# Token stream of the latent attention: its projections in a new order, with norms and rotations next to matmuls

## The reference, cut to what matters

```python
def _mla_q(h, w_dq, q_norm, w_uq, rows, cols):
    q = (_rms_norm(h @ w_dq, q_norm) @ w_uq).reshape(b, s, MLA_HEADS, MLA_NOPE + MLA_ROPE)
    q_nope, q_pe = q[..., :MLA_NOPE], q[..., MLA_NOPE:]
    q_pe = _rope_2d(q_pe, rows, cols)                     # token stream only
    return jnp.concatenate([q_nope, q_pe], -1)

def _mla_kv(h, w_dkv, kv_norm, w_ukv, rows, cols):
    ckv = h @ w_dkv
    c_kv, k_pe = ckv[..., :MLA_KV_RANK], ckv[..., MLA_KV_RANK:]
    kv = (_rms_norm(c_kv, kv_norm) @ w_ukv).reshape(b, s, MLA_HEADS, MLA_NOPE + MLA_V)
    k_nope, v = kv[..., :MLA_NOPE], kv[..., MLA_NOPE:]
    k_pe = _rope_2d(k_pe[:, :, None, :], rows, cols)      # token stream only
    k = jnp.concatenate([k_nope, jnp.broadcast_to(k_pe, (b, s, MLA_HEADS, MLA_ROPE))], -1)
    return k, v

# second block, layer 0: h = x * (1 + sc1) + sh1, and after the mixer
# x = layer_norm(alpha * x + g1 * y); softmax(q k^T * scale) v runs over context and token keys
```

## Time and profile before

| | |
|---|---|
| median of 3 runs | 2492.07 us |
| lowest, highest | 2491.98, 2493.27 us |
| profiled execution, its own time | 2489.5 us |
| span of the profiled execution | 2487.7 us |
| mean granted PE clock over the span | 0.954 |

### The profile page before, as it was taken

One profiled execution on the slowest core, in us unless ns is written; L12 is line 12 of the kernel. 1 busy time (PEld: TensorE's weight loads), 2 busy tenths in 40 slices (PEclk: granted clock), 3 DMA queues, 4 the chain that ended last, 5 costly groups with the idle time before them and its releaser, 6 DMA issues.

```text
span 2487.7 us, 29431 instructions
## 1 busy us (share of the span) xinstructions
PE 2161.0 (87%) x12748; PEld 1181.7 (48%) x12748; DVE 677.1 (27%) x1303; ACT 216.7 (9%) x507; POOL 41.3 (2%) x109
## 2 busy tenths in 40 slices
PE   8988889888768878878878876987889999999998
PEld 6544353333323334334334333434657776646775
DVE  1332211321310120120120123122444434165344
ACT  1221110000100000000000000002310000060000
POOL 0000000000000000000000000000000003000000
PEclk9999998989899999999999999998999999999999
DMA  8879999999999999999999999994337554424550
GB/s 321 328 291 396 420 408 424 424 423 422 424 421 418 416 420 414 416 420 413 414 421 416 414 424 422 391 417 179 132 100 226 183 189 161 154 75 144 168 171 34
DMA packets 154819, 799.52 MB, mean 321 GB/s; under 512 B 15587, under 2 KB 71626, under 8 KB 101634
## 3 DMA queue, kind: packets, MB, share of 16 engines
q1 hardware_dynamic: 144504, 783.43, 78.2%
q10 hardware_dynamic: 10186, 14.16, 1.7%
HBM read 795.40 MB, written 7.19 MB: 323 GB/s over the span
## 4 chain that ended last, share of the span: by engine, by line
PE 69%; DMA 17%; DVE 8%; issue 3%; ACT 2%; SPq 1%; ACTq 0%; DVEq 0%
PE ps L288 12%; PE ps L1992 9%; DMA ring<-in_mlp_w 8%; PE ps L2451 8%; PE ps L2443 8%; PE ps L321 6%; PE ps L1960 5%; PE ps L2162 4%; PE ps L1965 3%; PE ps L2013 2%; PE ps L2001 2%; DVE expert_work L2035 2%; DMA ring<-in_w_up 2%; DMA ring<-in_na_w_qkv 2%; DMA ring<-in_w_gate 2%
## 5 line engine op out<-in xcount | busy, mean ns | idle before, releaser
L1960 PE MATMUL ps<-ring,xe 128*32 128x512 f32 x2048 | 295.0, 638 | 80.7 <-DMA ring<-in_w_up 29.3
L1992 PE MATMUL ps<-ring,expert_work 128*32 128x512 f32 x1408 | 238.2, 691 | 11.8 <-ACT expert_work L2022 11.0
L1965 PE MATMUL ps<-ring,xe 128*32 128x256 f32 x2048 | 206.9, 462 | 6.0 <-issue 6.0
L1965 PEld LDWEIGHTS ps<-ring,xe 128*32 128x32 f32 x2048 | 74.9, 110 | 174.7 <-issue 174.0
L1960 PEld LDWEIGHTS ps<-ring,xe 128*32 128x32 f32 x2048 | 61.7, 114 | 186.2 <-issue 94.0
L1992 PEld LDWEIGHTS ps<-ring,expert_work 128*32 128x32 f32 x1408 | 59.7, 122 | 156.1 <-issue 132.8
L2162 PE MATMUL ps<-ring,c_qT 128*128 128x512 f32 x256 | 114.1, 598 | 12.1 <-DMA ring<-in_mlp_w 12.1
L2154 PE MATMUL ps<-hT,ring 128*128 128x256 f32 x512 | 115.0, 383 | 6.6 <-DMA ring<-in_mlp_w 6.6
L2451 PE MATMUL ps<-ring,mlp_x_h 128*128 128x512 f32 x256 | 112.3, 592 | 0.0
L2451 PE MATMUL ps<-ring,mlp_n_h 128*128 128x512 f32 x256 | 112.3, 592 | 0.0
L2154 PEld LDWEIGHTS ps<-hT,ring 128*128 128x128 f32 x512 | 96.2, 190 | 28.7 <-DMA ring<-in_mlp_w 11.0
(11 more groups left out here) (425 smaller groups left out, 2448.1 us busy)
## 6 DMA issues: line engine op xcount, KB each, us to landing
ring<-in_w_gate SPq DMA_DIRECT2D x128, 1408.0 KB, 16.8
ring<-in_w_up SPq DMA_DIRECT2D x128, 1408.0 KB, 17.4
ring<-in_w_down SPq DMA_DIRECT2D x112, 1536.0 KB, 22.8
ring<-in_mlp_w SPq DMA_DIRECT2D x96, 1024.0 KB, 8.1
ring<-in_ada_w SPq DMA_DIRECT2D x32, 1536.0 KB, 10.2
ring<-in_na_w_qkv SPq DMA_DIRECT2D x20, 1024.0 KB, 13.7
ring<-in_w_in SPq DMA_DIRECT2D x8, 1536.0 KB, 18.7
ring<-in_w_down SPq DMA_DIRECT2D x16, 512.0 KB, 23.5
```

What stands on the lines that cost most here:

```text
L1960: nc.tensor.matmul(ps[32 * j:32 * j + 32, up, :], xe[:, k, :], w[:, :, 4 * j:4 * j + 4], start=(k == 0), stop=(k == KC - 1))
L1965: last = nc.tensor.matmul(ps[32 * j:32 * j + 32, 2, 256 * up:256 * up + 256], xe[:, k, :], two, start=(k == 0 and not up), stop=(k == KC - ...
L1992: last = nc.tensor.matmul(ps[32 * j:32 * j + 32, 1 - half, :], hgT[:, at:at + 32], w[:, (c - c0) * D + 512 * half:(c - c0) * D + 512 * hal ...
```

## The change

The context stream's program stays as it is. For the token stream each engine gets one function of its own, and five things differ.

1. The query latent is normed alone: `square` of `cq` follows its evacuation, with a root for two columns, and the key/value latent gets a second, later norm. The junk output of the squares goes to `kT`.
2. `run_c` is split. `run_cq` (8 transposes of `cq`) uses banks 4 to 7 and waits for "norm_q" alone. `run_ckv` (6 transposes of `ckv`, `kpe`) uses banks 4 to 6.
3. `run_uq` is split. Its first 8 jobs run ahead of `run_ckv`, its last 2 jobs after it in banks 7 and 0. `run_ukv` follows in banks 4, 5, 6, 1, 2, 3.
4. `spread` gives all evacuations of `run_uq` and `run_ukv` to ACT: 22 of them, where ACT had 11.
5. DVE does the key/value norm, the key rotation, the gain on `x` and both rotations of `qpe` while PE runs the up projections. The key rotation's scratch is `va`.

```diff
-                self.run_c = Run(transposes(4, lambda t, c: cq[:, t, c * P:(c + 1) * P], lambda c: cqT[:, c, :],
+                queries_turned = transposes(4, lambda t, c: cq[:, t, c * P:(c + 1) * P], lambda c: cqT[:, c, :],
...
+                if s:
+                    self.run_c = Run(queries_turned + latents_turned, banks)
+                else:
+                    self.run_cq = Run(queries_turned, (4, 5, 6, 7))
+
+                def spread(i, out, scale=None, cols=None):
+                    if s:
+                        return turn(i, out, scale, None, cols)
+                    return to_act(out, 1.0 if scale is None else scale, 0.0, cols), "act"
...
-                self.run_uq = Run(jobs, banks)
+                if s:
+                    self.run_uq = Run(jobs, banks)
+                else:
+                    self.run_uq_most = Run(jobs[:8], banks)
+                    self.run_ckv = Run(latents_turned, (4, 5, 6))
+                    self.run_uq_rest = Run(jobs[8:], (7, 0))
...
-                self.run_ukv = Run(jobs, banks)
+                self.run_ukv = Run(jobs, banks if s else (4, 5, 6, 1, 2, 3))
...
+            def tokens_pe(self, pe, normed):
+                self.run_t.pe(pe, normed)
+                self.run_t.finished(pe)
+                self.run_d.pe(pe)
+                pe.wait_ge(self.v.sem, self.v.at("norm_q"))
+                self.run_cq.pe(pe)
+                self.run_cq.finished(pe)
+                self.run_d.finished(pe)
+                self.run_uq_most.pe(pe)
+                pe.wait_ge(self.v.sem, self.v.at("norms"))
+                self.run_ckv.pe(pe)
+                self.run_uq_most.finished(pe)
+                self.run_uq_rest.pe(pe)
+                self.run_ckv.finished(pe)
+                self.run_ukv.pe(pe)
+                self.run_uq_rest.finished(pe)
+                self.run_ukv.finished(pe)
+                pe.wait_ge(self.v.sem, self.v.at("rope_q"))
+                self.run_q.pe(pe)
+
+            def tokens_act(self, act):
+                cq, ckv, a, v = self.buf["cq"], self.buf["ckv"], self.a, self.v
+                junk = view(self.buf["kT"], 1, Q_RANK)[:, 0, :]
...
+                self.run_t.ev(act, "act")
+                for t in range(NT):
+                    self.run_d.ev(act, "act", t, t + 1)
+                    self.run_d.out_of(act, t)
+                    square(t, cq[:, t, :])
+                root(0, "var_q", "sd_q")
+                for t in range(NT):
+                    self.run_d.ev(act, "act", 2 + t, 3 + t)
+                    self.run_d.out_of(act, 2 + t)
+                    square(2 + t, ckv[:, t, 0:KV_RANK])
+                self.run_cq.ev(act, "act")
+                root(2, "var_kv", "sd_kv")
+                self.run_uq_most.ev(act, "act")
+                self.run_ckv.ev(act, "act")
+                self.run_uq_rest.ev(act, "act")
+                self.run_ukv.ev(act, "act")
+                self.run_q.ev(act, "act")
+
+            def tokens_dve(self, dve):
...
+                self.run_t.ev(dve, "dve")
+                self.run_d.ev(dve, "dve", 0, NT)
+                invert(0, Q_RANK, "sq1", "var_q", "sd_q")
+                for t in range(NT):
+                    last = nc.vector.tensor_scalar(cq[:, t, :], cq[:, t, :], small[:, t:t + 1], None, ALU.mult)
+                last.then_inc(v.sem, v("norm_q"))
+                self.run_d.ev(dve, "dve", NT)
+                self.run_cq.ev(dve, "dve")
+                invert(2, KV_RANK, "sq3", "var_kv", "sd_kv")
...
+                last.then_inc(v.sem, v("norms"))
+                dve.wait_ge(ln_loaded.sem, ln_loaded.n)
+                for t in range(NT):
+                    nc.vector.tensor_tensor(x[:, t, :], x[:, t, :], lnb[:, 0, :], ALU.mult)
+                self.run_ckv.ev(dve, "dve")
+                self.run_uq_most.finished(dve)
+                self.run_uq_rest.finished(dve)
...
+                last.then_inc(v.sem, v("rope_q"))
```

90 lines of the change are left out of this document (39 added, 51 removed).

## The result

The changed kernel takes 2479.4 us (median of 4 executions, 2476.7 to 2483.5) against 2492.7 us for the kernel before (median of 4, 2492.0 to 2494.1). The forecast was 2474.3 us with a range from 2470.5 to 2480.5.

A forecast was written before the change was run, and what follows sets the result against it. TensorE, busy for 87% of the span, was taken as the bound. The stage's terms sum to 46.3 us in place of 64.1, giving 2471.7 us profiled and, with 2.6 us for the median, 2474.3; range 2470.5 to 2480.5.

The forecast's parts named there:

- The sum: Down projection's end to the attention's first transposes: 46.3 us in place of 64.1, a gain of 17.8.
- the wait behind the transposes of `cq`: Before `run_uq`, PE waits 1.1 us for ACT's last square and two evacuations.
- the one for the last value tile: At the end of `run_ukv`, PE waits 0.7 us for ACT's last `va` evacuation; ACT alone otherwise costs nothing.
- the one ahead of the scores: After the `qpe` transposes, PE's wait for their last evacuation stays at 0.6 us.
- the eight transposes of `cq`: Right after the down projection, they start without a wait and take 1.1 us.
- The cover: `cq` norm done 5 us before PE arrives, under `ckv` matmuls; `qpe` rotation 9.6 us before, under `run_ukv`.
- The first scaled probabilities: At the attention's first transposes, their path fits into 3.0 us of scores; 0 to 1 us put on it.
- the point given as unknown: Clock across the stage's new short waits: taken to stay up, costing 0, with at most 5.7 us possible.
- the stages behind should last as long as now: After the changed stage, no later stage was to change its length, the MLP stage included.
- the gain is carried to the end: After the stage, nothing the next stage needs from DMA is late, so the 17.8 us reach the kernel's end.
- the clock rival: Clock falls at a short wait in the stage, keeping 3.3 to 5.7 us: 2477.6 to 2480.0 us; chance 0.12.
- An execution also varies by a microsecond or two: Whole kernel: executions were expected to differ by a microsecond or two, stated when setting the range.

The follow-up runs named there:

- before_third: The kernel before, unaltered, run once more for one profile; 2493.4 us (1 run).
- bridge: The changed kernel with four unread 512-column matmuls ahead of the output projection's 1.93 us wait; 2476.9 us (6 runs), ratio 0.9924 to 0.9962.
- the larger sample: The changed kernel, unaltered, measured a second time with more executions; 2477.4 us against 2494.0 for the kernel before.
- rope_beside: The kernel before with up-projection evacuations on ACT alone and `run_ukv` in its own banks, so DVE rotates `qpe` beside it; 2484.4 us (9 runs).
- before_again: The kernel before, unaltered, measured again; 2491.5 us (12 runs), ratio 0.9969 to 1.0000.
- tighter version: The changed kernel with `cq` transposes moved inside the down projection and `qpe` transposes ahead of the last two value jobs; 2471.0 us (4 runs).

## Why the prediction was right, and where it was off

**The sum.** 46.3 us were predicted for the stage and 45.7 measured, in all four executions. Term by term: the wait behind the transposes of `cq` 0.98 against 1.1, the one for the last value tile 0.73 against 0.7, the one ahead of the scores 0.61 against 0.6; two units of scores 1766.63 - 1760.69 = 5.9 against 6.0. The largest miss is that of the eight transposes of `cq`, 0.9 us up to the wait behind them against 1.1.

**The cover.** The norm of `cq` ended at 1715.4 where PE arrives at 1721.0, 5.6 us ahead (5 predicted). In times of this execution the prediction's 1710.9 would be 1715.7. The rotation ended at 1749.5 with PE arriving at its transposes at 1759.0, 9.5 us ahead (9.6 predicted). ACT evacuated `run_ukv` alone without delaying PE except at the end. The first scaled probabilities were in time: L680 follows the second unit's scores without idle time, so the 0 to 1 us put on that was 0.

**The clock in the stage.** It was the point given as unknown, between 0 and 5.7 us, and 0 was taken, by the start of the first MLP stage. It was 1.00 across waits of 0.98, 0.73 and 0.61 us, so the rival with a clock that falls at those waits did not occur there. That was one outcome of several that the rows left open, and the rows by which 0 was chosen vary themselves: in before_third the first MLP stage began behind a wait of 4.00 us instead of 1.83, and the same 16 matmuls took 3.33 us instead of 2.05. The Trainium skill, "TensorE: Matmul & The Clock Gate", section "A second HAM failure mode: psum-queue depth-cycling", has a swinging clock at short idles between groups. Through this stage's three short waits no such thing happened: the granted clock stood at 1.00 behind them in all four executions of the changed kernel and in bridge. At the output projection, behind 0.74 and 1.93 us, the clock fell once and came back in four of the five executions without long waits or filling.

**The step that failed** is "the stages behind should last as long as now", and with it "the gain is carried to the end". It was argued from DMA and from waiting, and there it holds: the waits of PE up to the first MLP stage are the same to 0.02 us. It left out that the clock can fall at a wait behind the stage whose length the change leaves as it is. The rivals had a fallen clock at the two places where the change leaves a wait, and none at a place that it doesn't touch. Whether the change brings that fall about or only met it stays open. The output projection's 1.7 us in four executions of five come to 1.4 on average. 18.4 - 1.4 = 17.0 is what the change would then give, against 16.7 measured in the larger sample.

The stage's gain and the medians' agree in the other kernels of the table too: 9.8 in the stage and 9.6 in the medians (rope_beside), 11.5 and 11.9, 5.8 and 5.7. In these three the output projection kept its 27.7. That they agree to 0.4 us is in part luck, as is the agreement of 17.0 and 16.7: two samples of the same program, before and before_again, differ by 2.5 us. For the tighter version 18.4 + 3.0 - 1.7 = 19.7 stands against 22.8 measured in four runs, whose interval reaches down to 19.5.

**The base.** The first measurement stands 5.1 us above the forecast. The profiled execution was to take 2471.7 us and took 2477.5, 5.8 more: the stage was 0.6 shorter, the output projection cost 1.5, and the slower time ahead of the stage 4.8. The median stands 1.9 us above the profiled execution, where the 2.6 of before were counted. "An execution also varies by a microsecond or two" was too small a figure: the three runs shown spread over 1.3 us, but 24 runs of before on one chip over 17. The median lay within the range by 1.1 us, but the range had been drawn for the clock rival, not for this spread: two of the four single runs, 2481.3 and 2483.5 us, lie above it. That the median of four held is in part luck.

## What to carry to other kernels

Norms and rotations on other engines belong beside the matmuls that don't need them, and what such a move is worth is PE's wait plus the slow clock behind it: here 12 us and 6. To learn the clock's share before rewriting anything, fill the wait with matmuls that nobody reads, counting two records for each float32 one. And where the gain is under one per cent, compare the stage's own rows first, and look for the rest in stages that the change didn't touch, since their clock can differ from run to run.

## What the runs showed of the chip

- Long waits are paid twice. 7.5 and 5.3 us of idle TensorE cost 5.8 us more behind them in the kernel before, but 0.9 and 1.1 us less than their share in the two kernels that had only one of them (one profiled execution each). The cost behind a wait of one length is not constant.
- The same program ran its first projection in 55.49 or in 58.2 to 58.5 us. Stretches of that projection, of the slow and of the fast case (columns as above, these matmuls alone), the first from the changed kernel:

```profile
20.00:22.00 2.00, 2.00 (x6) 1.57 (x5) 1.00 1.01 411
22.00:24.00 2.00, 2.00 (x6) 1.63 (x5) 1.00 0.98 408
24.00:26.00 2.00, 2.00 (x10) 1.77 (x10) 1.00 1.01 403
```

and the same stretches of bridge:

```profile
20.00:22.00 2.00, 2.00 (x11) 1.77 (x10) 1.00 1.01 411
22.00:24.00 2.00, 2.00 (x11) 1.77 (x10) 1.00 1.02 426
```

PE did 6 records in 2 us instead of 11, while the granted clock reads 1.00 in both and DMA is equally busy. It looks like the lower clock, but no row says so; either the record misses it at the program's start or something else halves the rate. That stays open.
- A wait of 1.93 us was followed by a clock of 0.50 in some executions and of 1.00 in others of the same kernel, and the clock ahead of it was 1.00 in both.
